# Attention with one fused pass for scores, position and maximum, a new order of its groups, and moved loads and tables, in a two-block transformer kernel

## What is computed

```
q = (h @ w_in)[..., :1024] * 64 ** -0.5          # 16 heads of 64, 4 key groups
gates = sigmoid((h @ w_in)[..., 1024:])          # 3 branches x 16 heads
s = q k_cmp - slope * distance                   # 15 compressed keys per group
o_cmp = masked_softmax(s) v_cmp
s = q k_slc - slope * distance                   # all 256 keys, since 4 blocks < 16
o_sel = masked_softmax(s) v_slc
s = q k_win - slope * distance                   # window of 512 holds all keys
o_win = masked_softmax(s) v_win
o = g0 * o_cmp + g1 * o_sel + g2 * o_win
y = o @ w_out
```

## Time and profile before

| | us |
|---|---|
| median of 3 runs | 2221.99 |
| lowest and highest | 2218.04 to 2227.21 |
| profiled execution | 2222.52 |
| span of its core | 2220.6 |
| mean granted clock | 0.968 |

### The profile page before, as it was taken

How to read it: one execution, slowest core, us unless ns; L and a number is a source line. 1 busy time by engine, 2 the same in 40 slices (tenths; PEclk the granted TensorE clock), 3 DMA queues, 4 the chain that set the end, 5 groups by cost and what they waited for, 6 DMA issues and landing times.

```text
span 2220.6 us, 39084 instructions
## 1 busy us (share of the span) xinstructions
PE 2119.6 (95%) x16942; PEld 2066.9 (93%) x16942; DVE 1587.5 (71%) x1865; ACT 1007.2 (45%) x1074; POOL 209.2 (9%) x342
## 2 busy tenths in 40 slices
PE   6999999999999997889998999999999999999997
PEld 5999999999999996689997999999999899998997
DVE  6777888877757777778879464758888546757655
ACT  3344646345443454544445463345445445335442
POOL 0111101111001111311101000001111000000000
PEclk8999999999789996999999999999999999999999
DMA  8899465996578843267976545464996645555652
GB/s 327 285 327 327 166 236 159 341 339 236 171 240 294 300 146 124 68 228 262 346 262 179 182 157 189 152 238 157 359 363 213 210 158 181 170 174 197 207 185 102
DMA packets 265386, 497.35 MB, mean 224 GB/s; under 512 B 17152, under 2 KB 146560, under 8 KB 264832
## 3 DMA queue, kind: packets, MB, share of 16 engines
q1 hardware_dynamic: 230192, 366.40, 49.4%
q0 software_dynamic: 35024, 128.47, 15.7%
HBM read 491.66 MB, written 1.05 MB: 222 GB/s over the span
## 4 chain that ended last, share of the span: by engine, by line
PE 79%; DVE 11%; DMA 5%; ACT 2%; issue 2%; SPq 0%; POOL 0%; DVEq 0%; ACTq 0%
PE PA L485 8%; PE PA L487 8%; PE PA L486 8%; PE PB L485 7%; PE PB L487 7%; PE PB L486 7%; PE PY L485 7%; PE PY L487 6%; PE PY L486 6%; DVE wlo L1320 3%; ACT whi L968 1%; DMA raw<-ffn_w_in 1%; DMA adaw<-adat 1%; DVE opA_lo L1405 1%; DMA raw<-w_ff 1%
## 5 line engine op out<-in xcount | busy, mean ns | idle before, releaser
L1320 DVE TENSOR_TENSOR wlo<-raw,whi 128x2048 fp32r<-128x2048 f32 x335 | 766.9, 2300 | 372.2 <-ACT whi L968 371.3
L968 ACT ACTIVATE whi<-raw 128x2048 fp32r<-128x2048 f32 x335 | 636.7, 1907 | 496.4 <-DMA raw<-ffn_w_in 199.4
L485 PE MATMUL PA<-opA_hi,whi 128*128 128x256 f32 x1344 | 382.0, 284 | 11.7 <-DVE opA_lo L1370 8.6
L485 PE MATMUL PY<-opB_hi,whi 128*128 128x256 f32 x1344 | 376.8, 280 | 4.6 <-DVE wlo L1320 3.9
L487 PE MATMUL PA<-opA_hi,wlo 128*128 128x256 f32 x1344 | 380.0, 283 | 0.0
L486 PE MATMUL PA<-opA_lo,whi 128*128 128x256 f32 x1344 | 378.9, 282 | 0.0
L487 PE MATMUL PY<-opB_hi,wlo 128*128 128x256 f32 x1344 | 375.0, 279 | 0.0
L486 PE MATMUL PY<-opB_lo,whi 128*128 128x256 f32 x1344 | 375.0, 279 | 0.0
L485 PE MATMUL PB<-opA_hi,whi 128*128 128x256 f32 x1216 | 342.9, 282 | 1.0 <-DVE wlo L1320 1.0
L487 PE MATMUL PB<-opA_hi,wlo 128*128 128x256 f32 x1216 | 342.0, 281 | 0.0
L486 PE MATMUL PB<-opA_lo,whi 128*128 128x256 f32 x1216 | 341.0, 280 | 0.0
(11 more groups left out here) (305 smaller groups left out, 3567.6 us busy)
## 6 DMA issues: line engine op xcount, KB each, us to landing
raw<-ffn_w_in SPq DMA_DIRECT2D x176, 512.0 KB, 5.3
scr<-adat POOLq DMA_DIRECT2D x150, 512.0 KB, 6.4
raw<-w_in SPq DMA_DIRECT2D x144, 512.0 KB, 4.6
raw<-w_ff SPq DMA_DIRECT2D x128, 512.0 KB, 4.8
adaw<-adat POOLq DMA_DIRECT2D x90, 512.0 KB, 6.2
raw<-ffn_w_out SPq DMA_DIRECT2D x88, 512.0 KB, 4.7
raw<-w_branch SPq DMA_DIRECT2D x48, 512.0 KB, 4.4
raw<-a_w_in SPq DMA_DIRECT2D x24, 512.0 KB, 4.4
```

Source lines behind the costliest of these rows:

```text
L485: nc.tensor.matmul(o_, w1, rhs(xh), start=start, stop=False, skip_group_check=True)
L968: AC(whi[slot][:, 0:w], raw[slot][:, 0:w], ACT.Copy).then_inc(hi_ready, 1)
L1320: TT(wlo[slot][:, 0:w], raw[slot][:, 0:w], whi[slot][:, 0:w].bitcast(F32), ALU.subtract).then_inc(lo_ready, 1)
```

## The change

1. `soft` becomes four fused instructions a unit: each adds the score block and the distance table times a constant, and takes the minimum at once. For this queries are divided by the slope (with the 1/8, in ScalarE's copy, table `qscale`), signs are turned, and the exponential has scale -1. The compressed scores are multiplied by the slope again (`cslope`, two instructions). PA and PB are released by the last of the four.
2. VectorE scales all four blocks in one instruction of 128x1024; GpSimd's 16 instructions and TensorE's wait for them are gone.
3. The nsa stage's order: chunks q0, q0, gates, q1, q1. The gate products go in halves of 128 tokens into spare columns of PB, and scores 0 to 2 stand between and behind the halves of q1. After unit 0's transposes TensorE runs 24 filler products (GAP_N). ScalarE's exponentials run two units ahead. The chunks of the output projection are prepared at units 5 and 8 of the loop.
4. adaLN: 40 slabs in ffn10 for 32, 8 in nsa for 16. Four of them are reduced behind the last unit, then the scales, then the last chunk. GpSimd no longer sends six slabs of ffn11 at the end of the attention.
5. The rotary angles (13 VectorE instructions, two sines), their table and the positions move from mix0 into ffn11.
6. In both mixers the three loads ws, bs and w_pool (1.5 MB) go from the fourth to the tenth group, and GpSimd adds its sums ahead of masking the gating weights.

```diff
+GAP_N = 24
...
-                                    ("ffn10", 24, 32), ("nsa", 32, 16), ("ffn11", 40, 40), ("ff0", 48, 48), ("ff1", 8, 8)):
+                                    ("ffn10", 24, 40), ("nsa", 32, 8), ("ffn11", 40, 40), ("ff0", 48, 48), ("ff1", 8, 8)):
...
+                    if name == "ffn11" and (kind, j) == ("in", 4):
+                        sp.wait_ge(multiplied, CH["nsa_out"] + 4)
+                        sp.dma_start(tb2, I["t_b2"]).then_inc(b2_in, 16)
+                        sp.dma_start(posi.bitcast(I32), I["positions"].partition_broadcast(P)).then_inc(b2_in, 16)
...
-                    if g == 3:
+                    if g == 9:
...
+            pe.wait_ge(lo_ready, c + 3)
             for k in range(KT):
-                o_ = flat["A"][0:48]
-                wh_, wl_ = whi[c % RING][:, k * 48:k * 48 + 48], wlo[c % RING][:, k * 48:k * 48 + 48]
-                nc.tensor.matmul(o_[:, 0:ZC], wh_, wide[:, k, :], start=k == 0, stop=False, skip_group_check=True)
-                nc.tensor.matmul(o_[:, 0:T], wh_, opl["A"][:, k, :], start=False, stop=False, skip_group_check=True)
-                last = nc.tensor.matmul(o_[:, 0:ZC], wl_, wide[:, k, :], start=False, stop=k == KT - 1, skip_group_check=True)
+                wh_, wl_ = whi[(c + 2) % RING][:, k * 48:k * 48 + 48], wlo[(c + 2) % RING][:, k * 48:k * 48 + 48]
+                for j in range(2):
+                    o_ = flat["B"][0:48, 512 * j + 260:512 * j + 388 + 2 * j]
+                    xh, xl = wide[:, k, P * j:P * j + P + 2 * j], opl["A"][:, k, P * j:P * j + P]
+                    nc.tensor.matmul(o_, wh_, xh, start=k == 0, stop=False, skip_group_check=True)
+                    nc.tensor.matmul(o_[:, 0:P], wh_, xl, start=False, stop=False, skip_group_check=True)
+                    last = nc.tensor.matmul(o_, wl_, xh, start=False, stop=k == KT - 1, skip_group_check=True)
             last.then_inc(multiplied, 1)
-            by("A", "V", "gate.z")
+            by("A", "V", "q0.z")
+            by("B", "V", "gate.z")
...
-                by(buf, "V", f"s{n_}")
-
+                by(buf, "V", f"m{n_}")
...
+            take("Y")
+            zchunk(c + 3, zbanks("Y"), tile_in512, range(0, 4), "11")
+            take("A")
+            need(pe, "S", "gate")
+            for ic in range(2):
+                last = nc.tensor.transpose(flat["A"][:, ic * 48:ic * 48 + 48], gfm[0:48, ic * P:ic * P + P], ident[0:48, 0:48])
+            S(last, "gt")
+            by("A", "S", "gexp")
             need(pe, "S", "q0")
             scores(0)
+            zchunk(c + 4, zbanks("Y"), tile_in512, range(4, 8), "11")
+            by("Y", "V", "q1.z")
+            scores(1)
+            scores(2)
...
+            scores(3)
+
+            def turn(n_):
+                ic = UNITS[n_][0]
+                need(pe, "V", f"p{n_}")
+                take("Y")
+                for jc in range(ic + 1):
+                    for x_ in range(4):
+                        last = nc.tensor.transpose(flat["Y"][:, (jc * 4 + x_) * P:(jc * 4 + x_ + 1) * P],
+                                                   ssb[n_ % 3][:, x_, jc * P:jc * P + P], ident)
+                S(last, f"pt{n_}")
+                by("Y", "S", f"pt{n_}")
+
+            turn(0)
+            for _ in range(GAP_N):
+                nc.tensor.matmul(PY[:, 4, 0:P], ident, onesD, start=True, stop=True)
...
+            for n_ in range(1, len(UNITS)):
+                if 3 < n_ + 2 < len(UNITS):
                     scores(n_ + 2)
-                need(pe, "V", f"p{n_}")
-                need(pe, "G", f"p{n_}")
-                take("Y")
-                for jc in range(ic + 1):
-                    for x_ in range(4):
-                        last = nc.tensor.transpose(flat["Y"][:, (jc * 4 + x_) * P:(jc * 4 + x_ + 1) * P],
-                                                   ssb[n_ % 3][:, x_, jc * P:jc * P + P], ident)
-                S(last, f"pt{n_}")
-                by("Y", "S", f"pt{n_}")
-                if n_:
-                    weighted(n_ - 1)
+                turn(n_)
+                weighted(n_ - 1)
...
+            exps(0)
+            exps(1)
+            zcopy("q1", [qf[:, 4 + m, :] for m in range(4)], qscale[:, 4:8])
+            exps(2)
+            for ic in range(2):
+                need(act, "V", f"csub{ic}")
+                S(AC(pc32[:, ic, :, 0:N_CMP], sc_[:, ic], ACT.Exp), f"cexp{ic}")
+            turned(0)
+            need(act, "T", "pct")
+            S(AC(ptc.rearrange("p i r c -> p (i r c)"), flat["Y"][:, 0:1024], ACT.Copy), "ptc")
+            for n_ in range(1, 16):
+                if n_ + 2 < 16:
+                    exps(n_ + 2)
+                turned(n_)
+                if n_ in (4, 7):
+                    prep_to(c + (7 if n_ == 4 else 8))
...
                 if n_ >= 3:
                     need(dve, "T", f"pt{n_ - 3}")
                 for u in range(2):
-                    h = (2 * a + u) * R + r
-                    v = S(STT(ssb[n_ % 3][:, 2 * u:2 * u + 2, 0:W], dist[:, T - W:T].unsqueeze(1).broadcast_to([P, 2, W]),
-                              sl_[h], PS["BA"[n_ % 2]][:, 2 * u:2 * u + 2, 0:W], ALU.mult, ALU.add), f"s{n_}")
-                own(v)
-                S(nc.vector.tensor_reduce(small[:, 4 * (n_ % 3):4 * (n_ % 3) + 4], ssb[n_ % 3][:, :, 0:W], AX.X, ALU.max,
-                                          negate=True), f"m{n_}")
+                    for b_ in range(2):
+                        x_ = 2 * u + b_
+                        S(nc.vector.tensor_tensor_reduce(ssb[n_ % 3][:, x_, 0:W], PS["BA"[n_ % 2]][:, x_, 0:W], dist[:, T - W:T],
+                                                         -sl_[(2 * a + u) * R + r], 3.0e38, ALU.add, ALU.min,
+                                                         accum_out=small[:, 4 * (n_ % 3) + x_:4 * (n_ % 3) + x_ + 1]), f"m{n_}")
+
+            def scaled(n_):
+                ic, a, r = UNITS[n_]
+                rs = small[:, 80 + 4 * (n_ % 3):84 + 4 * (n_ % 3)]
+                W = (ic + 1) * P
+                need(dve, "S", f"e{n_}")
+                own(S(nc.vector.reciprocal(rs, small[:, 96 + 4 * (n_ % 3):100 + 4 * (n_ % 3)])))
+                gt = gates[:, ic, 16:48].rearrange("p (b h) -> p h b", b=2)[:, r * 4 + 2 * a:r * 4 + 2 * a + 2, :]
+                S(TT(t3(rs, 2), t3(rs, 2), gt, ALU.mult), f"rs{n_}")
+                own(S.n)
+                S(TT(ssb[n_ % 3][:, :, 0:W], ssb[n_ % 3][:, :, 0:W], rs.unsqueeze(2).broadcast_to([P, 4, W]), ALU.mult), f"p{n_}")
 
...
+            scaled(0)
+            soft(1)
+            ada_to(nsa0 + 4)
+            prep_to(c + 6)
+            need(dve, "S", "q0")
+            dve.wait_ge(multiplied, c + 5)
+            zevac("q1", "Y")
+            settle()
+            S(TT(zb[:], zb[:], qscale[:, 4:8], ALU.mult), "q1.z")
+            scaled(1)
+            soft(2)
...
+            soft(3)
+            for n_ in range(2, 16):
+                scaled(n_)
                 if n_ + 2 < 16:
                     soft(n_ + 2)
-                if n_ == 1:
-                    prep_to(CH["nsa_in"] + 8)
-                if n_ >= 2:
-                    out_split(n_ - 2)
+                if n_ in (5, 8):
+                    prep_to(c + (7 if n_ == 5 else 8))
+                out_split(n_ - 2)
             out_split(14)
             out_split(15)
-            prep_to(CH["nsa_out"] + 3)
-            ada_to(nsa0 + 12)
+            ada_to(nsa0 + 8)
+            mods("nsa")
...
-            ada_send(nsa0 + 8)
+            ada_send(nsa0 + 4)
             S(pool.memset(pc32[:, :, :, N_CMP:32], 0.0), "ppad")
-            for n_ in range(16):
-                W = P if n_ < 8 else T
-                rs = small[:, 80 + 4 * (n_ % 3):84 + 4 * (n_ % 3)]
-                need(pool, "V", f"rs{n_}")
-                S(pool.tensor_tensor(ssb[n_ % 3][:, 2:4, 0:W], ssb[n_ % 3][:, 2:4, 0:W],
-                                     rs[:, 2:4].unsqueeze(2).broadcast_to([P, 2, W]), ALU.mult), f"p{n_}")
             ada_send(sum(RUN["nsa"]))
             pool.wait_ge(ada_used, ADA0["ffn11"][0])
             pool.dma_start(crow[:], I["c_rows"][1:2].partition_broadcast(P)).then_inc(crow_again, 16)
-            need(pool, "V", "olo15")
-            ada_send(ADA0["ffn11"][0] + SLABS)
...
+                for h in range(4):
+                    need(pool, "S", f"b{l}.osq{h}")
+                    S(pool.tensor_tensor(t3(rr, 4)[:, h, :], tmp8[:, 2 * h, :], tmp8[:, 2 * h + 1, :], ALU.add), f"b{l}.osum")
```

171 lines of the change are left out of this document (71 added, 100 removed).

## The result

The changed kernel takes 2204.95 us (median of 6 runs, 2198.87 to 2208.81), the kernel before 2224.27 on the same chips. The ratio is 0.991, with a 95% interval of 0.9891 to 0.993. The forecast was 2204. So the change makes the kernel 0.9% faster, as a sum whose terms can now be read one by one. The medians differ by 19.3 us. The spans of the two profiled executions, from which all that follows is read, fall from 2220.6 to 2203.6, by 17.0.

What follows compares the result with a forecast made beforehand. TensorE, busy 2119.6 of 2220.6 us, was taken as the bound, leaving its idle or low-clock time to win. Attention 0, boundary -9.0, ffn11 -0.6, mix0 -6.2, mix1 -2.6 sum to -18.4 against 2222.5: 2204.1 us, range 2199 to 2210.

Steps and rivals of the forecast that it cites:

- Boundary: Attention's output projection to the next stage's first group: the wait on the accumulator and low clock behind it go, -9.0 us.
- Attention: First group of the attention stage to its output projection: no net change, 0 us, bounds -3 and +8.
- the loop's ring: Attention loop: TensorE, soft step, four exponentials, copy and handovers in one chain, 8.2 us for two 256-key units.
- the wait: TensorE idle ahead of the compressed scores in the attention: 8.1 us, scores starting at about 855.0.
- 4.2 and 2.3 us: Attention loop, units 5 and 8: cost of the two chunk splits, where nothing hides them.
- rival of a dearer fused instruction: Soft step: 0.5 us or more for 256 elements, ring 8.8, +4, total 2208; counted within the forecast's range.
- The slower rival: Half clock through the whole attention, a 256-key unit costing TensorE nearly 7 us, total 2226; chance 0.05.
- clock early: Attention: clock rises 6 us after the wait's end, at 861, projection at 928.7, total 2201; chance 0.1.
- mix0: First mixer: angles no longer ahead of a split -4.0, half clock -2.6, some 0.4 back: -6.2 us, bounds -3.5 and -7.
- mix1: Second mixer: loads moved to group 9 no longer delay the half swap's DMA, -2.6 us, bounds 0 and -3.
- ffn11: Start of the feed-forward stage behind the attention: split and mods ahead, -0.6 us, bounds -2 and +1.5; angles there 0.
- Eight slabs more in ffn10: Stage before the attention: 9.8 us more VectorE work and 4 MB, costing 0, bound +2.

Runs made afterwards that it cites:

- The shift in the kernel before: Kernel before with 40 slabs in ffn10, 8 in nsa, the new end and no early GpSimd sends, nothing else of the change: 2211.06 us, ratio 0.9953.
- the reordered base: Changed kernel with the second query group evacuated before unit 1's soft step and the loop's two splits moved behind the last unit: 2194.39 us, ratio 0.9865.
- the run with the early loads: Changed kernel with the gating and pool weights loaded at the fourth group of both mixers again, masking ahead of the sums: 2214.21 us, ratio 0.9951.

## Why the prediction was right, step by step

**Boundary (-9.0, measured -8.57): right, and shown but for one point.** The shift in the kernel before gives -7.5 there; how much of it is due to the slabs that GpSimd no longer sends early is not shown. The two later pairs' loading was priced rightly (9 us into the projection, measured 945.0 - 936.7 = 8.3). What the step missed is the other gain of the same edit: it nowhere named the two slabs fewer ahead of the second group, and they were worth 4.2 us in the attention of before. The forecast counted the old 5.05 wait as given and priced the new order absolutely, so the sum was not hurt.

**Attention (0, measured +2.25): the terms right up to unit 1, the loop's ring right, one term short.** Price of the fused step (0.35), of the wait (8.1, measured 8.69) and the rise of the clock during the fillers came out as worked, and 8.19 for the 8.2 of two units. Unit 1 turned 1.1 us sooner than forecast. From there to the projection the forecast had 57.7 us, and it took 61.1. Of the 3.4 too much, 2.5 is the term "4.2 and 2.3 us" for the two splits, which measured 9.0 together: the second cost 4.7, since the waits behind the splits brought the clock down twice, which the term lacked. The other 0.9 stands in the loop without splits too (52.1 us for 51.2), on the way to the first 256-key unit (20.8 for 19.5). In the kernel before, the forecast read 28.0 for the seven steps and 25.9 for the three pairs; they are 27.1 and 26.9, but only the sum is used. The forecast's rival of a dearer fused instruction did not come. Nor did the fixed extra of the Trainium skill's "VectorE: DVE Perf Modes" (errata section): the estimate from its 150 cycles, 0.42 us for each 256-wide instruction, is the row's duration, but the instructions started 0.34 to 0.35 apart, and it is that which counts.

**Its own signs.** The forecast said that a slow clock past the fillers would make it wrong. It came: half clock for 3.4 and 6.8 us in the loop. So the account of the attention was wrong there, though the total was met. The slower rival (half clock through the loop) has this small part of truth. The clock did not fall behind the loop's own short waits of about 1 us but behind waits of 3. The waits in the mixers, 1.26 and 1.56, also stayed above the "1 us or less" that it named.

**The clock.** "What they buy is the clock" was right in mechanism (half clock until 866 with fillers, until 880 without, in the times of before) and nearly idle in value: 0.3 to 2.2 us in the changed kernel, 1.3 in the reordered base. The rise was counted from the end of the compressed scores, which the runs bear out: with fillers the clock is full again 4 us behind the scores' end in the changed kernel and 6 in the reordered base, and it rose within the scores in none of the runs. The rival *clock early* did not come in any run. The rule behind it, that activity releases the throttle ("TensorE: Matmul & The Clock Gate", section "What's actually happening", of the Trainium skill), disagrees with the 7 busy us of the compressed scores at half clock as it did at 590.

**mix0 (-6.2, measured -6.26): size right, cause half told.** The step that failed is "The angles stood ahead of that split: -4.0", and with it the -2.6 of half clock: all of the gain was put to the angles. The runs show that angles and loads each hold the same 6.4 us: had only the angles moved, the term would have been 0. The comparison with mix1, on which the step rested, hid this, since mix1 at the loads' old place lost its 3 us at another product. And the angles' way to the split led over ScalarE's rounding, not over VectorE's order.

**mix1 (-2.6, measured -2.86): right in cause and direction.** The size has luck in it: the new code took 77.3 to 80.7 in eleven kernels, the old 81.51, 83.42 and 83.85 in three.

**ffn11 (-0.6, measured -0.30): not shown.** The same code took 193.2 to 196.1 elsewhere. That the 13 angle instructions cost nothing there is shown: 193.22 with them and 193.22 without.

**Eight slabs more in ffn10 (0, measured -0.1 over 268 us): right.** A price of w_pool at the tenth group (0 to +2) was not seen, in a stretch that scatters by over 6 us.

**The rest.** That the total met the forecast to 1 us is partly luck: -15.7 of the named terms and -1.3 of the clock's scatter elsewhere, against -18.4 forecast. The attention alone would have given 1.9 less in another execution of the same code.

## What to carry to other kernels

Cut both traces at the same products and compare stretches: single runs of the whole scatter by 4 us and more, while a stretch that meets no change of clock repeats to 0.1. Where the clock can fall, a stretch scatters too, by 2 to 3 us here, and it takes more than one execution to read it. Two delays that hold the same consumer must both go before either shows, and the price of a wait on TensorE is more than its length when it is long enough to bring the clock down. Running a producer further ahead on an engine that also makes the urgent copy puts that work in the copy's way: one unit less ahead was worth 4.3 us.

## What the runs showed of the hardware that was not expected

- Waits of about 3 us in a loop (2.93, 3.02) were followed by half clock for 3.4 us in some executions of the same code and for 6.8 or 10 in others. Waits of 1 to 1.65 us in every unit were not, in the kernels with the fused step and no splits in the loop, nor were those of 2.0 in the run with the early loads; with the old soft step, whose units are longer, waits of 1.65 and 2.56 were.
- The clock fell inside the compressed scores although TensorE had waited only 0.61 us ahead of them and had no gap within: two windows of the kernel before with the slabs' shift.

```profile
850.10:853.00 2.90, 2.90 (x54) 2.90 (x54) 2.90 (x5) 0.01 (x1) 0.00 (x0) 1.00 1.00 364
853.40:854.40 1.00, 1.00 (x12) 1.00 (x11) 0.91 (x2) 0.98 (x2) 0.00 (x0) 0.50 0.09 37
```

- The clock after an equal wait of 1.89 us at the same place of the same code was full in one execution and half in another, worth 1.5 us. That such places make most of the scatter of the totals is not shown.
- The fused add-and-minimum with its accumulator read starts every 0.34 us at 256 elements and every 0.21 us at 128, though each shows a duration of 0.42 and 0.29.
